# Expert gates: one-hot matmuls replaced by indirect accumulating DMAs into a zeroed DRAM array

## What is computed

```python
q = einsum('td,dhq->thq', xt, w_pq)                  # 8 heads, two halves of 128
s1, s2 = q1 @ keys1.T, q2 @ keys2.T                  # 128 scores each
v1, i1 = top_k(s1, 16); v2, i2 = top_k(s2, 16)
cand = v1[:, None] + v2[None, :]                     # 16 x 16
sc, ci = top_k(cand, 16)
eid = i1[ci // 16] * 128 + i2[ci % 16]               # one of 16384 experts
gate = softmax(sc)
hid = gelu(einsum('td,thkd->thk', xt, expert_u[eid]))
out = einsum('thk,thkd->td', gate * hid, expert_v[eid])
```

## Time and profile before

| | us |
|---|---|
| median of 3 runs | 2120.8 (2117.65 to 2122.53) |
| span of the profiled execution, first to last instruction | 2115.7 |
| PE busy in it | 2016.0 (95%) |
| DVE busy | 1619.7 (77%) |
| ACT busy | 794.0 (38%) |
| POOL busy | 552.0 (26%) |

### The profile page before, as it was taken

How to read it: one execution, slowest core, us unless ns; L and a number is a source line. 1 busy time by engine, 2 the same in 40 slices (tenths; PEclk the granted TensorE clock), 3 DMA queues, 4 the chain that set the end, 5 groups by cost and what they waited for, 6 DMA issues and landing times.

```text
span 2115.7 us, 33945 instructions
## 1 busy us (share of the span) xinstructions
PE 2016.0 (95%) x12943; PEld 1845.7 (87%) x12943; DVE 1619.7 (77%) x3030; ACT 794.0 (38%) x1311; POOL 552.0 (26%) x334
## 2 busy tenths in 40 slices
PE   8998889889999999999999999999989899999998
PEld 8998879778756999999999999999978787778786
DVE  6635767564355327999999799999979888989888
ACT  4335453432331322322344444444433333333332
POOL 0000020000000000212112055555547656656540
PEclk9999889999999999999999999999999999999999
DMA  5223210151550403768667488999999999999993
GB/s 171 89 93 116 86 47 1 41 204 42 191 208 21 160 1 121 261 232 285 223 219 270 140 290 330 338 346 340 337 381 387 386 387 387 383 385 384 375 377 113
DMA packets 223185, 483.75 MB, mean 229 GB/s; under 512 B 11984, under 2 KB 137168, under 8 KB 221415
## 3 DMA queue, kind: packets, MB, share of 16 engines
q1 hardware_dynamic: 176998, 314.56, 41.9%
q0 software_dynamic: 46080, 167.79, 21.8%
HBM read 423.29 MB, written 58.36 MB: 228 GB/s over the span
## 4 chain that ended last, share of the span: by engine, by line
PE 43%; DMA 8%; DVE 5%; SPq 3%; issue 1%; ACT 1%; DVEq 0%; ACTq 0%
PE ps L2599 9%; PE ps L2595 9%; PE ps L2991 8%; PE ps L2594 8%; DMA raw_v<-peer_v 6%; PE ps L2585 5%; PE ps L2623 4%; SPq L2969 3%; DVE kept L3100 3%; DVE v_high_low L3163 1%; DVE outputs L3157 1%; DMA outputs<-hidden 1%; ACT v_high_low L3057 0%; DMA kept<-peer_v,kept 0%; SPq L2967 0%
## 5 line engine op out<-in xcount | busy, mean ns | idle before, releaser
L2991 PE MATMUL ps<-v_high_low,gated_high_low 128*128 128x512 f32 x2304 | 532.9, 393 | 22.0 <-ACT gated_high_low L3059 18.3
L2991 PEld LDWEIGHTS ps<-v_high_low,gated_high_low 128*128 128x128 f32 x2304 | 435.8, 190 | 119.0 <-ACT v_high_low L3057 15.0
L2594 PE MATMUL ps<-x_high_low,u_high_low 128*128 128x384 f32 x1024 | 356.3, 348 | 0.0
L2595 PE MATMUL ps<-x_high_low,u_high_low 128*128 128x384 f32 x1024 | 345.6, 337 | 0.0
L3083 POOL DMA_INDIRECT outputs<-peer_v,kept x138 | 264.2, 1914 | 170.0 <-DVE kept L3100 137.3
L2711 POOL DMA_INDIRECT scores<-peer_u,kept x64 | 94.0, 1468 | 729.3 <-DVE kept L2831 552.4
L2669 ACT ACTIVATE kept<-ps 128x384 f32<-128x384 f32 x128 | 62.9, 491 | 407.5 <-PE ps L2599 398.0
L2599 PE MATMUL ps<-x_high_low,u_high_low 128*128 128x384 f32 x1024 | 204.7, 341 | 0.0
L2595 PEld LDWEIGHTS ps<-x_high_low,u_high_low 128*128 128x128 f32 x1024 | 193.3, 189 | 0.0
L2594 PEld LDWEIGHTS ps<-x_high_low,u_high_low 128*128 128x128 f32 x1024 | 193.0, 189 | 0.0
L3163 DVE TENSOR_TENSOR v_high_low<-raw_v,v_high_low 128x1024 fp32r<-128x1024 f32 x120 | 146.3, 1219 | 51.1 <-ACT v_high_low L3057 51.1
(11 more groups left out here) (471 smaller groups left out, 4113.9 us busy)
## 6 DMA issues: line engine op xcount, KB each, us to landing
experts<-peer_u SPq DMA_DIRECT2D x63, 1024.0 KB
raw_v<-peer_v SPq DMA_DIRECT2D x60, 1024.0 KB
hidden<-kept SPq DMA_DIRECT2D x64, 384.0 KB
gates<-scores SPq DMA_DIRECT2D x12, 2048.0 KB, 9.4
first_hidden<-hidden SPq DMA_DIRECT2D x16, 768.0 KB, 18.4
outputs<-gates SPq DMA_DIRECT2D x16, 768.0 KB
outputs<-hidden SPq DMA_DIRECT2D x16, 768.0 KB, 15.4
first_gates<-gates SPq DMA_DIRECT2D x15, 768.0 KB
```

The costliest lines, as they stand in the source:

```text
L2594: pe.matmul(o, utr[:, b, HI, k], xr[:, HI, k, 0:DN], start=(k == 0), stop=False)
L2595: pe.matmul(o, utr[:, b, HI, k], xr[:, LO, k, 0:DN], start=False, stop=False)
L2991: ins = pe.matmul(bank(c, 2 * t + h), gr[:, slot, x, DN * b + P * t:DN * b + P * t + P], vr[:, slot, y, D * b + 512 * h:D * b + 512 * h + ...
```

## The change

Five things:
- A DRAM array of gates, of 128 rows by 128 x 384, is filled with zeros in the delta phase: POOL clears 4096 columns, SP stores them 12 times. A wait for these stores stands in ACT's part of the mix phase.
- In place of pairs turned over, one-hots, products, copies and stores of the gates, DVE computes the softmax and, for each pair, the place of its gate in the array (place). POOL then adds, for each of the 3 x 128 pair columns, 128 gates of 4 bytes through 128 indices with an accumulating indirect DMA. Before each head of 16 columns it waits until all earlier ones of that tile have landed.
- The same POOL queue fetches rows of u between heads: 4 after each head of tile 0, none in tile 1, 12 in tile 2, and the last 44 after all scatters. The ring has 8 buffers.
- Picks run in the order 0, samples, 1, 2, 3. The samples' scores keep only the copy's own quarter of the heads, so that their pick handles 32 pairs. Low parts come every 3.9 units. After the picks the dots left are spread over the low parts left.
- The gates and the hidden values both lie in DRAM with 384 contiguous words per block, so that a load of four blocks is one run per partition.

The core of the diff (the changed shapes inside pick are left out):

```diff
+ZEROS = 4096
+DENSE = NT - 2
+DN = DENSE * P
+GATE_ROW = NK * DN
+def gate_rows(c):
+    return c.gates_dram.rearrange("p g k t -> p (g k t)")
+def gate_blocks(c):
+    return gate_rows(c).rearrange("p (b t) -> p b t", t=DN)
+def hidden_blocks(c):
+    return c.hidden_dram.rearrange("p b t -> p (b t)")[:, 0:GATE_ROW].rearrange("p (b t) -> p b t", t=DN)
...
@@ phase_delta, sync
             sp.dma_start(s_s[:].rearrange("p b h v -> p (b h) v"), d.state_dn[0].rearrange("b h k v -> k (b h) v")).then_inc(states_in, 16)
+            sp.wait_ge(zeros_set, 1)
+            for i in range(GATE_ROW // ZEROS):
+                sp.dma_start(gate_rows(c)[:, ZEROS * i:ZEROS * i + ZEROS], zeros).then_inc(c.gates_zeroed, 16)
             sp.wait_ge(uw, NT)
...
         def _(pool):
+            pool.memset(zeros, 0.0).then_inc(zeros_set, 1)
...
@@ phase_cross, scalar
+            act.wait_ge(c.gates_zeroed, 16 * (GATE_ROW // ZEROS))
             act.copy(xh[:, 0:4, SEQ:TOK], sample_mix).then_inc(x_hi, 1)
...
@@ phase_scores, vector
-                        ins = v.tensor_copy(sc[:, 4, 2 * h:2 * h + 2], bank(c, 6, 256).rearrange("p (j k) -> p j k", j=2))
+                        r, j = slice(SAMP * (h // 2), SAMP * (h // 2) + SAMP), 2 * (h % 2)
+                        ins = v.tensor_copy(sc[r, 4, j:j + 2], bank(c, 6, 256)[r].rearrange("p (j k) -> p j k", j=2))
...
-RING = len(SLOTS)
+RING = len(SLOTS) + 3
...
-GATES_AT = 25
-DOT_EVERY, LOW_EVERY = 2.2, 4.7
-DOTS_BY = {4: 0, GT: 16, 0: 32, 1: 46, 2: 59}
+PICKS = (0, 4, 1, 2, GT)
+DIVIDED = {0: 1, 1: 2, 2: 3, 4: 4, GT: 5}
+EXPS_AT = {0: 7, 1: 21, 2: 29, GT: 37}
+DOTS_BY = {0: 0, 4: 0, 1: 24, 2: PAIRS_EACH, GT: PAIRS_EACH}
+ROWS_PER_HEAD = {0: 4, 1: 0, 2: 12}
+DOT_EVERY, LOW_EVERY = 2.2, 3.9
...
@@ phase_hidden, sync
+            looped(sp, 3, NQ - 5, NQ - 3, group)
+            sp.wait_ge(picked, NT)
+            for e in range(2):
+                sp.dma_start(v_first[:, 2 * e:2 * e + 2], v_rows[:, 2 * e:2 * e + 2]).then_inc(c.first_v, 16)
+            group(NQ - 3, (NQ - 3) % 2)
+            sp.wait_ge(gates_exp, NT)
+            sp.wait_ge(spots_set, DENSE)
+            for i in range(2):
+                sp.wait_ge(hid_stored[i], 16)
+            sp.dma_start(hid_first, hidden_blocks(c)[:, 0:4]).then_inc(c.first_gated, 16)
+            group(NQ - 2, (NQ - 2) % 2)
+            group(NQ - 1, (NQ - 1) % 2)
+            for n in range(DENSE):
+                sp.wait_ge(scattered[n], 16 * PAIRS)
+            sp.dma_start(gates_first, gate_blocks(c)[:, 0:4]).then_inc(c.first_gated, 16)
+            store(NQ - 1, (NQ - 1) % 2)
...
@@ phase_hidden, tensor
+            looped(pe, 3, NQ - 3, NQ, group)
...
@@ phase_hidden, scalar
+            def exps(n):
+                act.wait_ge(picked, order[n] + 1)
+                act.activation(gates_of[n], kept[:, n, 2, 0:pairs_of(n)], ACT.Exp).then_inc(gates_exp, 1)
...
+            span(act, 3, EXPS_AT[0], group)
+            exps(0)
+            span(act, EXPS_AT[0], EXPS_AT[1], group)
+            exps(4)
+            exps(1)
...
@@ phase_hidden, gpsimd
+            def fetch(upto):
+                for no in range(fetched[0], min(upto, ROWSETS)):
+                    if no == 0:
+                        pool.wait_ge(ids_set, 1)
+                    if no == PAIRS_EACH:
+                        pool.wait_ge(ids_set, 2)
+                    after(pool, row_used, no - RING + 1)
+                    pool.indirect_dma_start(out=ring[no % RING], out_offset=None, in_=d.peer_u[0],
+                                            in_offset=bass.IndirectOffsetOnAxis(ap=ids[:, no:no + 1], axis=0)).then_inc(row_in[no % RING], 16)
+                fetched[0] = max(fetched[0], upto)
+            def add_gates(n, h):
+                after(pool, scattered[n], 16 * TOPK * h)
+                for i in range(TOPK * h, TOPK * h + TOPK):
+                    pool.indirect_dma_start(out=all_gates, out_offset=bass.IndirectOffsetOnAxis(ap=spot[:, n, i:i + 1], axis=0),
+                                            in_=gate[:, n, i:i + 1], in_offset=None, compute_op=ALU.add).then_inc(scattered[n], 16)
+            for n in range(DENSE):
+                if n == 1:
+                    fetch(PAIRS_EACH)
+                pool.wait_ge(spots_set, n + 1)
+                for h in range(PH):
+                    add_gates(n, h)
+                    if h + 1 < PH:
+                        fetch(fetched[0] + ROWS_PER_HEAD[n])
+            fetch(ROWSETS)
...
@@ phase_hidden, vector
+            def place(n):
+                divided(n)
+                step(v.scalar_tensor_tensor(at_row, kept[:, n, 1], float(NK), kept[:, n, 0], ALU.mult, ALU.add))
+                step(v.tensor_scalar(at_row, at_row, float(DN), token[:, n:n + 1], ALU.mult, ALU.add))
+                v.tensor_copy(spot[:, n], at_row).then_inc(spots_set, 1)
...
+            left = ROWSETS - dots[0]
+            more, start = NK - lows[0], dots[0]
+            for i in range(more):
                 low()
+                while dots[0] < start + left * (i + 1) // more:
                     dot()
...
@@ phase_combine
-                sp.dma_start(gt[slot].rearrange("p g b t -> p g (b t)"),
-                             c.gates_dram[:, :, bass.ds(g * GB, GB)].rearrange("p g b t -> p g (b t)")).then_inc(g_in[slot], 16)
-                sp.dma_start(ht[slot], c.hidden_dram[:, bass.ds(g * GB, GB), 0:DN]).then_inc(h_in[slot], 16)
+                sp.dma_start(gt[slot], gate_blocks(c)[:, bass.ds(g * GB, GB)]).then_inc(g_in[slot], 16)
+                sp.dma_start(ht[slot], hidden_blocks(c)[:, bass.ds(g * GB, GB)]).then_inc(h_in[slot], 16)
```

More of the change, by code:

```diff
@@ L2567, in _, with group @@
+                sp.dma_start(hidden_blocks(c)[:, bass.ds(q * UG, UG)], hid[:, slot]).then_inc(hid_stored[slot], 16)
+            def group(q, slot):
+                if not isinstance(q, int) or 0 < q and q + 1 < NQ:
+                    load(q + 1, 1 - slot)
+                if not isinstance(q, int) or q > 0:
+                    store(q - 1, 1 - slot)
             load(1, 1)
@@ L2586, in turn, with hidden @@
                 ins.then_inc(turned, 1)
-            def hidden(n, b, between, afterwards):
+            def hidden(n, b):
                 pe.wait_ge(ut_kept, n + 1)
@@ L2626, in sums_of_gates, with group @@
-            def sums_of_gates():
-                pe.wait_ge(exps, 1)
-                pe.matmul(bank(c, 6, DN), one_head, gate, start=True, stop=True).then_inc(sums, 1)
+            def group(q, slot):
+                for b in range(UG):
+                    n = q * UG + b
+                    if b == 0:
+                        turn(n + 1, slot, 1)
+                    elif not isinstance(q, int) or q + 1 < NQ:
+                        pe.wait_ge(u_in[1 - slot], loads(q + 1, 1 - slot) - 16 * slot)
+                        turn(n + 1, 1 - slot, 0)
+                    hidden(n, b)
@@ L2690, in _ @@
[L2690 to L2699 removed]
+                group(q, q % 2)
@@ L2778, in pick @@
-                step(v.tensor_tensor(c3[:, :, 9], b2[:, 0, :, 8:16], b2[:, 1, :, 0:1].broadcast_to([P, PH, 8]), ALU.add))
-                between(1.8, upto)
-                t3, p3 = (x.rearrange("p (h k) -> p h k", h=PH) for x in (top, pair))
-                best16(lambda g: cand[:, g], lambda g: t3[:, g], lambda g: p3[:, g], PH, 0.3, upto)
+                r, heads = pairs_of(n), pairs_of(n) // TOPK
+                part = r / PAIRS
+                top, pair, hi, lo, hif, lof = (row[0][:, 0:r], *(x[:, 0:r].bitcast(U32) for x in row[1:4]), row[4][:, 0:r], row[5][:, 0:r])
@@ new lines, in pick @@
+                tail, second = row[2][:, 0:r], row[3][:, 0:r]
+                places = words(c, H_B + 512, 2, PAIRS)[:, :, 0:r]
+                best16(lambda g: sc[:, n, g], lambda g: best[:, g], lambda g: where[:, g], 2 * heads, 0.35, upto)
+                v.tensor_copy(keys16[:, 0:2 * r].rearrange("p (g k) -> p g k", k=16), where[:, 0:2 * heads])
+                b2 = best[:, 0:2 * heads].rearrange("p (h s) k -> p s h k", s=2)
+                few = cand[:, 0:heads]
+                c3 = few.rearrange("p h (r k) -> p h r k", k=8)
@@ new lines, in pick @@
+                v.tensor_tensor(few[:, :, 0:16], b2[:, 0, :, 0:1].broadcast_to([P, heads, 16]), b2[:, 1], ALU.add)
+                v.tensor_tensor(c3[:, :, 2:9], over(b2[:, 0, :, 1:8], 3, [P, heads, 7, 8]), over(b2[:, 1, :, 0:8], 2, [P, heads, 7, 8]), ALU.add)
+                step(v.tensor_tensor(c3[:, :, 9], b2[:, 0, :, 8:16], b2[:, 1, :, 0:1].broadcast_to([P, heads, 8]), ALU.add))
+                between(1.8 * part, upto)
+                t3, p3 = (x.rearrange("p (h k) -> p h k", k=TOPK) for x in (top, pair))
@@ L2836, in _ @@
-            step(v.scalar_tensor_tensor(tail, kept[:, GT, 0], float(NK), kept[:, GT, 1], ALU.mult, ALU.add))
-            v.tensor_copy(ids[:, PAIRS_EACH:], tail).then_inc(ids_set, 1)
-            for n in range(3):
-                pick(n, DOTS_BY[n]).then_inc(picked, 1)
```

(29 more changed lines are left out.)

297 lines of the change are left out of this document (71 added, 226 removed).

## The result

The kernel after takes 2485.6 us (median of 4 runs, 2479.2 to 2491.3) against 2119.8 us before on the same chip: a ratio of 1.172, 95% interval 1.170 to 1.175. It is slower by 366 us. The forecast was 2214 us with a range of 2020 to 2340, so the sign was right, and the size lay outside the range. The profiled execution took 2486.4 us, its span is 2484.7.

What follows compares the result with a forecast made beforehand. PE was taken to bound the kernel before, and POOL's scatter queue to delay it after. Hidden phase +108 us and contiguous arrays -15 gave +93 on 2120.8, so 2214 us; range 2020 to 2340.

Steps and rivals of the forecast that it cites:

- (b): Hidden phase: 384 scatters on POOL at 1.24 us each delay rows of u; phase ends at 1656 us, +108.
- port term: Hidden phase: DVE's dots hold up POOL's fetches, 0.2 us a dot, 25 us taken, range 0 to 121.
- landing waits in tile 1: Hidden phase: POOL waits 7 times for a head's scatters to land, 22 us, or 54 with loaded queues.
- tail of 44 rows: End of hidden phase: dots tied to low parts stretch the last 44 rows over 19.6 blocks, 99 us.
- the accumulate doubles POOL's work: Rival for the scatters on POOL: reading old values makes each 2.18 us, kernel 2575 us, half of it 2395; chance 0.15.
- a scatter step near 2 us: Sign against the forecast, in POOL's scatters: would put the DMA side, not POOL, in charge.
- The cheap rival: Scatters on POOL much cheaper than fetches: 2074 us at 0.94 us each, 2014 at 0.79 and below; chance 0.33.
- (a): Hidden phase: without one-hots PE loses 86 us and some 3 more, giving a floor of 1459 us for its end.
- (c): Picks, exps and table loads in the hidden phase: DVE's savings and ACT's extra work hide, counted at nothing.
- (d): Delta phase: storing 25 MB of zeros takes 113 us but stays hidden, counted at nothing, at most 9 us.
- (e): Combine phase: contiguous arrays give longer load runs and save 15 us, bounds 0 and 18.

Runs made afterwards that it cites:

- no_scatter: The kernel after with the scatters and the waits for them left out, gates of tiles 0 to 2 staying zero: 2029.5 us.
- both_contiguous: The kernel before, one-hots kept, with the hidden and gates arrays both laid out contiguous for the load of four blocks: 2102.0 us, ratio 0.9919.

## Why the prediction was wrong

**The step that failed** is the price of a scatter in part (b): "I see no reason to price it lower, and take 1.24 us", the fetch's price for an operation that also adds. It measured 1.94. The terms of that sum, forecast and measured:

| term | forecast | measured |
| --- | --- | --- |
| first scatter | 890 | 893.0 |
| 384 scatters, without and with the port term | 476 to 501 | 384 x 1.94 = 746 |
| 116 fetches | 144 | 32 x 1.26 + 84 x 1.555 = 171 |
| landing waits in tile 1 | 22 | 17.6, and 3.9 for tile 1's places |
| last scatter done | 1557 | 1832.5 |
| tail of 44 rows | 99 | 109 |
| hidden phase ends | 1656 | 1942 |

The measured terms add up to 1832, as read. Of the 286 us between the ends, 245 to 270 are the scatter's, by where the 25 us for dots are counted.

**The rival that was nearest** was "the accumulate doubles POOL's work": 2395 us for half of the extra work, 2575 for all. The extra is 0.59 us on 0.95, and 2486 lies between them. It had a chance of 0.15, and the range was cut just below it. The sentence against it, "nothing in the trace", was no evidence against: the trace of before had no adding transfer at all, so it could not speak on the point. The Trainium skill, page "Collectives: The Full Stack", section "The bandwidth ceiling", says that an add takes two read descriptors for each chunk where a copy takes one. The trace agrees only in that an adding transfer makes more of them: an adding scatter left 144 packets on POOL's queue (101376 less the 46080 of no_scatter, over 384), a plain one 32, which is more than a doubling. Nor do the packets price the add: with 64 indices in place of 128 an adding scatter has 64 packets fewer (80) and is 0.14 us shorter, so 112 more packets would be some 0.25 us by that slope, of the 0.59. What POOL does in the rest is open.

That the DMA side and not POOL would be in charge at "a scatter step near 2 us", as the prediction's last part has it, did not come so either: the step is POOL's own busy time, and the waits for landings in tile 1 were 1.7 to 3.9 us a head.

**The cheap rival** (2014 to 2074 us, chance 0.33) needed a scatter of under 1.06 us. Even the plain scatter has a step of 1.26, and at that step it runs into the second limit, which no term of the forecast had. The argument against this rival, that the fetch's floor "looks like a cost per index", was wrong in its reason: half the indices made a plain scatter 0.06 us shorter (0.89 against 0.95), so it is nearly all a cost per instruction.

**(a)** The floor of 1459 us: no_scatter ended its hidden phase at 1485. Its first low-part products stood 6.8 us later than before (821.8 against the earlier trace rows), and it had 10 us of waits more than the kernel before. The working of the floor holds within some 9 us.

**(c)** At nothing: right as far as seen. In no_scatter PE had no gap from 950 to 1150 us and from 1200 to 1450, with picks, exps and table loads in their new places.

**(d)** At nothing: right. SP issued the twelve stores from 276.7 us on and w_o at 386.38, where the earlier trace rows had 389.10. But the estimate of 113 us for 25 MB was long: the DMA engines moved them at some 430 GB/s, until about 342 us.
```profile
276.69 20.23 SPq L1080 DMA_DIRECT2D gates<-kept  x12
386.38 0.39 SPq L1082 DMA_DIRECT2D layer<-w_o  x1
```

**(e)** 15 us expected, bounds 0 and 18; measured 23 in the kernel after (552.5 to 529.5) and 21 in both_contiguous. That lies above the upper bound, since PE's own 534 us was worked out with three extra products beside the 4.13 us a block; the phase is 5 us shorter than that. The queues' side, from 2000 to 2350 us:
```profile
DMA packets 35689, 143.79 MB, mean 411 GB/s; under 512 B 3346, under 2 KB 3346, under 8 KB 35682
```
against 385 GB/s and 50690 packets under 2 KB in the earlier trace rows. By the rule of the Trainium skill, page "DMA: Bandwidth & Descriptors", section "Specifications", that 512 B is enough for full rate, the layout was to give nothing. The trace disagrees by 6% or more: mixed loads in runs of 512 B and 1.5 KB went at 385 GB/s with PE waiting for them, runs of 6 KB at 411 with PE full, which may be all that PE asks for.

## What to carry to other kernels

An operation that the trace does not show has its price from the nearest row only for what it shares with it; for what it does more (here the add) the dear end deserves as much weight as the near one. Before indirect DMAs are moved onto POOL, count them: here each cost 0.94 us plain and 1.54 adding, with 0.30 between them, most of it per instruction, and a full queue shows as some 80% busy. Long batches of the cheap kind need spacing (2395 us with it, 2463 without), or PE loses what POOL gains. What another engine waits for goes ahead of a long batch in the same queue: 128 scatters cost 142 us in heads of 16 and 26 us spread. And the part of a change that pays can be had without the rest: the layout alone, with the one-hots kept, gives 0.8%.

## What the runs showed of the hardware

- An indirect DMA of 128 indices held POOL 0.94 us for 4096 bytes an index and 0.94 for 4. An adding scatter held it 1.54 us with 128 indices and 1.40 with 64; a plain one 0.95 and 0.89.
- Where POOL issued 128 indices in 1.24 to 1.26 us (102 a us) about ten times or more in a row, PE's own instructions came late: 1.4 to 2.8 us apart beside plain scatters, with the DMA engines 5% busy, and with gaps of up to 1.1 us behind ten to twelve fetches, of 4 KB rows or of single words. At 81 a us and below nothing of it was seen. The cause is open.
- An adding scatter of 128 indices left 144 packets on POOL's queue and one of 64 left 80; a plain one left 32 with either.
- The DMA engines' rate in the combine phase rose from 386 to 411 GB/s (PE then had no gap) with runs of 6 KB in place of 512 B and 1.5 KB.
